# Where a streamed operand and the weights lie in SBUF, modulo 512 bytes, in a two-layer hybrid model

## The reference, cut to what matters

```
for i in range(DEPTH):
    h = rms_norm(x, ffn1_norm[i])
    x = x + 0.5 * swiglu(h, ffn1_w_gate[i], ffn1_w_up[i], ffn1_w_down[i])
    ...                                    # even_mixer or odd_mixer
    h = rms_norm(x, ffn2_norm[i])
    x = x + 0.5 * swiglu(h, ffn2_w_gate[i], ffn2_w_up[i], ffn2_w_down[i])
```

## Time and profile before

| | us |
|---|---|
| median of 2 runs | 1904.78 (1904.30 to 1905.25) |
| the profiled execution | 1904.64 |
| its span, first to last instruction | 1902.8 |
| granted TensorE clock, mean | 0.998 |

### The profile page before, as it was taken

How to read it: one execution, slowest core, us unless ns; L and a number is a source line. 1 busy time by engine, 2 the same in 40 slices (tenths; PEclk the granted TensorE clock), 3 DMA queues, 4 the chain that set the end, 5 groups by cost and what they waited for, 6 DMA issues and landing times.

```text
span 1902.8 us, 31445 instructions
## 1 busy us (share of the span) xinstructions
PE 1872.6 (98%) x11916; PEld 1668.0 (88%) x11916; DVE 1458.7 (77%) x2330; ACT 1021.4 (54%) x1640; POOL 194.8 (10%) x251
## 2 busy tenths in 40 slices
PE   7999999999999999999999999999999999999999
PEld 6899899888779899998889989887778789899997
DVE  8879587577679788597877859756989878687684
ACT  7546264477776355364645526455456766364451
POOL 1311010000001011010011101011111001011010
PEclk9999999999999999999999999999999999999999
DMA  7666662211137565563465546166765376565441
GB/s 241 155 200 183 174 167 64 100 67 67 56 111 183 167 169 146 150 173 109 134 170 156 152 143 179 45 165 161 167 153 131 86 200 170 158 183 161 133 112 67
DMA packets 94789, 271.66 MB, mean 143 GB/s; under 512 B 10504, under 2 KB 10760, under 8 KB 94640
## 3 DMA queue, kind: packets, MB, share of 16 engines
q1 hardware_dynamic: 63456, 201.22, 30.7%
q0 software_dynamic: 29232, 64.50, 19.3%
q10 hardware_dynamic: 1952, 3.93, 1.1%
HBM read 223.07 MB, written 2.77 MB: 119 GB/s over the span
## 4 chain that ended last, share of the span: by engine, by line
PE 88%; DVE 7%; ACT 3%; issue 2%; DMA 0%; DVEq 0%; ACTq 0%
PE ps_unit L814 13%; PE ps_unit L815 13%; PE ps_unit L816 13%; PE ps_y L878 6%; PE ps_y L877 6%; PE ps_y L879 6%; PE ps_s L877 4%; PE ps_s L878 4%; PE ps_t L878 4%; PE ps_t L877 4%; PE ps_t L879 4%; PE ps_s L879 4%; PE ps_s L814 1%; DVE cv L2479 1%; PE ps_s L815 1%
## 5 line engine op out<-in xcount | busy, mean ns | idle before, releaser
L1423 ACT ACTIVATE gw_hi<-gu 128x512 fp32r<-128x512 f32 (+1 forms) x400 | 319.0, 799 | 151.5 <-PE ps_s L879 69.3
L1954 DVE TENSOR_TENSOR gw_lo<-gu,gw_hi 128x512 fp32r<-128x512 f32 (+1 forms) x400 | 354.6, 901 | 46.5 <-ACT gw_hi L1423 35.0
L814 PE MATMUL ps_unit<-a_hi,w_hi 128*128 128x512 f32 x892 | 351.0, 394 | 5.4 <-DVE w_lo L1885 2.8
L815 PE MATMUL ps_unit<-a_lo,w_hi 128*128 128x512 f32 x892 | 348.0, 390 | 0.0
L816 PE MATMUL ps_unit<-a_hi,w_lo 128*128 128x512 f32 x845 | 329.2, 390 | 0.0
L1358 ACT ACTIVATE w_hi<-raw 128x1024 fp32r<-128x1024 f32 (+1 forms) x125 | 125.3, 1003 | 305.1 <-PE ps_unit L816 301.4
L814 PEld LDWEIGHTS ps_unit<-a_hi,w_hi 128*128 128x128 f32 x892 | 167.6, 188 | 44.3 <-DVE w_lo L1885 5.1
L2091 DVE TENSOR_TENSOR t<-ps_unit,half 128x512 f32<-128x512 f32 x96 | 66.4, 691 | 172.8 <-PE ps_unit L816 172.4
L815 PEld LDWEIGHTS ps_unit<-a_lo,w_hi 128*128 128x128 f32 x892 | 167.6, 188 | 32.8
L816 PEld LDWEIGHTS ps_unit<-a_hi,w_lo 128*128 128x128 f32 x845 | 158.6, 188 | 33.8
L879 PE MATMUL ps_y<-xu_hi,gw_lo 128*128 128x256 f32 x640 | 180.5, 282 | 0.0
(11 more groups left out here) (324 smaller groups left out, 4648.7 us busy)
## 6 DMA issues: line engine op xcount, KB each, us to landing
gu<-gu_stream_dram SPq DMA_DIRECT2D x176, 512.0 KB, 5.1
raw<-w_stream_dram SPq DMA_DIRECT2D x136, 512.0 KB, 3.3
gu<-gu_stream_dram SPq DMA_DIRECT2D x80, 256.0 KB, 3.0
gu<-gu_stream_dram POOLq DMA_DIRECT2D x80, 256.0 KB, 4.0
gu<-gu POOLq DMA_DIRECT2D x80, 256.0 KB, 3.3
w_lo<-raw POOLq DMA_DIRECT2D x28, 512.0 KB, 4.9
raw<-w_stream_dram SPq DMA_DIRECT2D x32, 384.0 KB, 3.5
w_lo_3rd<-raw POOLq DMA_DIRECT2D x15, 512.0 KB, 4.7
```

Of the source, the lines that this page charges most:

```text
L814: pe.matmul(ps, lhs_hi, rhs_hi, start=first, stop=False)
L815: pe.matmul(ps, lhs_hi, rhs_lo, start=False, stop=False)
L1423: act.activation(gw_hi[:, w, :], src, ACT.Copy).then_inc(gw_hi_done, 1)
L1954: dve.tensor_tensor(gw_lo[:, w, :], src, gw_hi[:, w, :].bitcast(F32), ALU.subtract).then_inc(gw_lo_done, 1)
```

## The change

The two pads of 64 bytes are taken out, so `xu_lo`, `xt` and `xs` lie at `xu_hi`'s offset modulo 512, and a pad of 192 bytes is put in ahead of `stage`, so that `gw_hi` and `gw_lo` lie 256 bytes from them modulo 512. No instruction is added, removed or moved.

```
-HALF_LINE = 64
+STAGE_PAD = 192
...
         low = top[0]
         xu_hi = sb("xu_hi", [P, PAIRS, 3 * TH], F32R)
-        top[0] += HALF_LINE
         xu_lo = sb("xu_lo", [P, PAIRS, 3 * TH], F32R)
-        top[0] += HALF_LINE
         low_top = top[0]
...
         head_sel = sb("head_sel", [P, 2])
+        top[0] += STAGE_PAD
         stage = top[0]
         gu = sb("gu", [P, 11, PIECE])
         gw_hi = sb("gw_hi", [P, 7, PIECE], F32R)
```

## The result

The changed kernel takes 1929.37 us (median of 2 runs, 1928.72 to 1930.02) against 1904.78: ratio 1.0129, 95% interval 1.0086 to 1.0173. It is slower by 24.6 us, where I had forecast 17 us faster. The profiled execution's span is 1926.9 us (before 1902.8), at the same granted clock, 0.998.

The account below looks back on a forecast made before the run. TensorE's own pace was taken to bound the FFN phases. 80 hidden tiles at 0.20 us less (16.0 us) plus 1 us from plain tiles made -17 us, from 1904.64 to 1888 us; range 1883 to 1918.

Parts of the forecast that it names:

- What bounds the kernel: FFN phases: only TensorE's own pace sets the end, with matmuls filling 98% of the span.
- two readings: Matmul pace: either any constant distance lets load and stream settle (taken), or certain distances are good by themselves.
- The attention rows: Attention products at distances 0 and 256 by turns: 0.12 us each, three after each change, judged not to decide.
- The -12.1 us for `xu`: FFN hidden tiles: 2880 `xu` matmuls go from 117.5 to 113.3 ns each, a gain of 12.1 us.
- The plain tiles: 384 matmuls of 512 columns on `xs` and `gw`, distance 64 to 256: at best 2.6 us gained, 1 us taken.
- Rival 1: 256-column products: 256 is a bad distance, 120 ns each, 1933 us, or mildly 117.5, 1917 us; chance 0.20.
- Rival 2: `xu` matmuls are slower for a reason other than addresses, so the time stays at 1905 us; chance 0.07.
- The bound below: 256-column matmuls can't come faster than the weight load's 112 ns; the forecast's low end is set at 1883 us.

Follow-up runs that it names:

- run 2: Changed kernel without its 192-byte pad and with a 64-byte tensor moved from above x to below it, distance 0 for all of x: 1929.0 us, ratio 1.0130.
- run 1: Changed kernel with the 192-byte pad ahead of the stage region left out, distance 64 for all of x: 1912.8 us, ratio 1.0043.
- runs 5 and 6: Kernel of run 1 plus one extra matmul, 64 or 128 columns, starting each FFN phase's second and third groups: 1891.8 and 1891.5 us.

## Why the prediction was wrong, point by point

- **What bounds the kernel, which classes change, and that nothing else moves**: right. The 384 and 6720 matmuls carry all of the difference but 1 or 2 us, which are shifts of waits, and the units keep 226.7 ns.
- **The step that failed** is the choice between two readings: "Either a constant distance is what lets load and stream fall into a rhythm in which they don't meet (then 256 is as good as 64 in the 256-column products)". Settling is real, but what the stream can settle to is a property of the distance: 120 at 0 and 256, 118.7 or 120 on average at 128, 113.3 or 117.8 at 64 and 192. The change had a constant distance everywhere and lost on every matmul of 256 columns. I had held that a good distance reached by accident "would be luck". It was luck in part, and in part the two pads of 64 bytes, which kept `xs` in the faster of its two rhythms.
- **The attention rows** The earlier trace rows had the answer, three steps of 0.12 at distances 0 and 256. I set them aside because `xs` also needs some matmuls at a switch; run 2 and the kernel after show that 0.12 is the settled pace at both distances.
- **The -12.1 us for `xu`** rested on the same step: it came out as 2880 x (120.0 - 117.8) = +6.3 us. `xs` came out as 3840 x (120.0 - 114.7) = +20.4, 114.7 being its mean step in the trace before, switches included.
- **The plain tiles**: at best 2.6 gained, 1 taken; some 2.4 by their settled steps, 1.5 with their waits. The sign was right, and 256 equals 0 there.
- **Rival 1** is what happened, and its pace of 120 was exact. Its 1933 us is 4 too high: it leaves the plain tiles' 2.4 out, and 80 tiles at 9.72 are 777.6 us, 2 less than the 779.7 that the trace has. It deserved more than 0.20. Its threshold, a settled pace above 115.7 ns, decided as stated: 120 lies above it.
- **Rival 2**, addresses are not the cause, fell: 0, 64, 128 and 256 differ by up to 17 us, with the same instructions in the same order. By the rule of the Trainium skill (TensorE: Matmul & The Clock Gate, Step-by-step), that loading the next weights takes no read bandwidth from the running matmul, the addresses should not matter; these runs show that they do (6720 matmuls at 120.0 ns in run 2, at 117.2 in run 1), whatever the mechanism.
- **The bound below** was sound: no run has a settled pace under 113.3. Nine tenths of the 6720 matmuls can have it, and that gives 1892 us in runs 5 and 6, near the 1888 that I had forecast; but by distance 64 and an odd matmul, not by the change.

What stays open: which part of SBUF or of TensorE's fetch makes the distance count, why an odd matmul turns the slow rhythm of distance 64 into the fast one behind down units and does the reverse behind some plain tiles, and why it does not at 192. The runs show that it does, not how. Distances 384 and 448 were not run; by the period of 256 they would be those of 128 and 192.

## What to carry to other kernels

Where TensorE is busy all the time, measure the step from start to start of each class of matmuls, and put the differences beside the distance, modulo 256 bytes, between the streamed operand and the weights that load meanwhile: 6% of a matmul's step lay there, and pads of 64 bytes move it. The good distance depends on the number of columns (of those tried 64 gave the best times for 256 columns, 0 and 256 the best pace for 512), so measure it at the width at hand and don't reason from another. A stream can also sit in the slower of two rhythms until something odd passes by, so a row that is "settled" proves nothing for another distance or another entry. Look through the whole trace for short stretches at another pace before you say that a distance has only one.

## What the runs showed of the hardware that was not expected

- The step of a 128x128 by 256-column matmul, weights loaded for each, settles at fixed values: 113.3 or 117.8 ns (distances 64, 320 and 192), 120.0 (0 and 256), 118.7 or 120.0 on average (128), 118.4 (32); with 512 columns 226.7 (distances 0 and 256), some 229 (192), 232 (128) and 233.3 (64 and 32).
- The same instructions at the same addresses run at 113.3 or at 117.8 ns for hundreds of matmuls; one extra matmul of 64 columns (step 0.03 us) ahead of each of the two later groups of a phase, 8 in the kernel, saves 21 us.
- Distances 64 and 320 behave alike, and 0 and 256: the period is 256 bytes.
